# A hybrid decoder step on one core: sample sequences divided into front and back between mixed prompt items, with their products four heads beside each other

## What is computed

```python
s_c = einsum('bqkgd,bnkd->bqkgn', q, kc) * scale - sl * d_c      # compressed blocks
o_c = einsum('bqkgn,bnkd->bqkgd', masked_softmax(s_c), vc)
s_s = einsum('bqkgd,bqknld->bqkgnl', q, ks) * scale - sl * d_s   # selected blocks
o_s = einsum('bqkgnl,bqknld->bqkgd', masked_softmax(s_s), vs)
s_w = einsum('bqkgd,btkd->bqkgt', q, kw) * scale - sl * d_w      # window
o_w = einsum('bqkgt,btkd->bqkgd', masked_softmax(s_w), vw)
o = g[..., 0:1] * o_c + g[..., 1:2] * o_s + g[..., 2:3] * o_w    # gates
y = o @ w_o
```

## Time and profile before

| | us |
|---|---|
| median of 3 runs (1967.68 to 1974.69) | 1971.83 |
| the profiled execution, its own time | 1970.03 |
| its span, first to last instruction | 1968.4 |
| of this, the attention stage (1109.1 to 1441.3) | 332.2 |

### The profile page before, as it was taken

How to read it: one execution, slowest core, us unless ns; L and a number is a source line. 1 busy time by engine, 2 the same in 40 slices (tenths; PEclk the granted TensorE clock), 3 DMA queues, 4 the chain that set the end, 5 groups by cost and what they waited for, 6 DMA issues and landing times.

```text
span 1968.4 us, 30231 instructions
## 1 busy us (share of the span) xinstructions
PE 1714.8 (87%) x12401; PEld 1514.8 (77%) x12401; DVE 917.9 (47%) x1631; ACT 558.4 (28%) x1053; POOL 271.3 (14%) x384
## 2 busy tenths in 40 slices
PE   4789973579999999989898987878898999999995
PEld 2666652479999999979888754444487999999994
DVE  1489999664323222353234445544535323323333
ACT  2322221433221122222213533433423322122212
POOL 1003938020000000001100323232300000000000
PEclk7889986799999999998999988778688999999997
DMA  9399971061232223312312301010121223222311
GB/s 323 135 355 330 329 267 46 0 154 55 85 106 74 69 86 92 91 54 68 89 43 79 112 23 44 22 44 1 49 59 44 86 86 104 69 76 86 96 45 48
DMA packets 236591, 198.10 MB, mean 101 GB/s; under 512 B 6999, under 2 KB 196127, under 8 KB 236253
## 3 DMA queue, kind: packets, MB, share of 16 engines
q1 hardware_dynamic: 230448, 172.54, 28.5%
q0 software_dynamic: 5840, 23.30, 3.8%
q10 hardware_dynamic: 173, 0.39, 0.1%
HBM read 188.88 MB, written 11.20 MB: 102 GB/s over the span
## 4 chain that ended last, share of the span: by engine, by line
PE 70%; DVE 12%; issue 8%; ACT 4%; DMA 2%; DVEq 1%; POOL 1%; SPq 0%; ACTq 0%; POOLq 0%
PE ps L1422 56%; PE ps L1404 4%; PE ps L1730 3%; DVE y L1096 1%; PE ps L1806 1%; DMA ada<-in_w_ada_dram 1%; PE ps L1609 1%; DVE wl L950 1%; DVE r L1096 1%; PE ps L1450 1%; DVE Pp L1241 1%; DVE r L974 1%; ACT Pp L862 1%; POOL Pp L592 1%; PE ps L1694 1%
## 5 line engine op out<-in xcount | busy, mean ns | idle before, releaser
L1422 PE MATMUL ps<-Hh,wh 128*128 128x288 f32 x2128 | 469.5, 303 | 65.5 <-DVE Hl L989 40.8
L1422 PE MATMUL ps<-Hl,wh 128*128 128x288 f32 x2128 | 464.9, 301 | 0.0
L1422 PE MATMUL ps<-Hh,wl 128*128 128x288 f32 x2128 | 463.7, 300 | 0.0
L629 ACT ACTIVATE wh<-raw 128x1024 fp32r<-128x1024 f32 (+1 forms) x173 | 192.8, 1116 | 818.6 <-PE ps L1422 798.3
L1422 PEld LDWEIGHTS ps<-Hh,wh 128*128 128x128 f32 x2128 | 350.3, 193 | 69.5 <-issue 68.2
L1422 PEld LDWEIGHTS ps<-Hl,wh 128*128 128x128 f32 x2128 | 351.1, 193 | 0.2
L1422 PEld LDWEIGHTS ps<-Hh,wl 128*128 128x128 f32 x2128 | 350.5, 193 | 0.2
L950 DVE TENSOR_TENSOR wl<-raw,wh 128x1024 fp32r<-128x1024 f32 (+1 forms) x173 | 225.1, 1301 | 255.1 <-ACT wh L629 254.6
L1422 PE MATMUL ps<-al,wh 128*128 128x288 f32 x704 | 151.0, 296 | 0.0
L1422 PE MATMUL ps<-ah,wl 128*128 128x288 f32 x704 | 150.9, 296 | 0.0
L1422 PE MATMUL ps<-ah,wh 128*128 128x288 f32 x704 | 150.9, 296 | 0.0
(11 more groups left out here) (267 smaller groups left out, 2033.4 us busy)
## 6 DMA issues: line engine op xcount, KB each, us to landing
ada<-in_w_ada_dram SPq DMA_DIRECT2D x64, 1024.0 KB, 7.7
raw<-in_ffn_w_up_dram SPq DMA_DIRECT2D x88, 512.0 KB, 3.8
raw<-in_ffn_w_down_dram SPq DMA_DIRECT2D x32, 704.0 KB, 4.6
raw<-in_conv_w_pw_dram SPq DMA_DIRECT2D x24, 512.0 KB, 8.3
raw<-in_w_kv_dram SPq DMA_DIRECT2D x12, 512.0 KB, 3.8
C<-in_cache_kv_dram POOLq DMA_DIRECT2D x32, 128.0 KB, 4.3
raw<-in_nsa_w_in_dram SPq DMA_DIRECT2D x8, 512.0 KB, 3.8
Cs<-in_cache_kv_dram SPq DMA_DIRECT2D x16, 256.0 KB, 3.8
```

Source lines behind the costliest of these rows:

```text
L629: A(wh[:, u % RING, 0:K, 0:w], raw[:, u % RING, 0:K, 0:w], ACT.Copy).then_inc(hi_ready, 1)
L1422: last = M(ps[0:w, 2 * s + h, 0:HT], wt[:, s, k, 0:w], rt[:, k, h * HT:(h + 1) * HT], start=(k == 0 and i == 0), stop=(k == K - 1 and i == 2))
```

## The change

Three things change, all in the attention stage.

1. **The plan.** Prompt items come in a mixed order (`PROMPTS`; i = 1, 3, 3, 1, 1, 2, 3, 0, 3, 0, 2, 0, 2, 1, 2, 0). Sample sequences are no items of the pipeline any more: a front (`s_keys` twice, `s_score`, `s_weigh`) and a back (`s_turn` twice, `s_prod`, `s_oturn`) are placed each in the slot of a given prompt step (`SMP_FRONT`, `SMP_BACK`), spread among what is left of the item ahead after its first four entries. Those four stand one by one between the new item's four scores and `cmp`. `weigh` stands four entries later.
2. **The product.** The turned weights are stationary (32 columns), values move (64 columns), and four heads write 32 PSUM partitions each, beside each other. The result [128, 64] is copied to `So` (DVE), transposed back (`s_oturn`), and written to `oTs` in two copies by DVE or ACT.
3. **Buffers and the end.** `Cs` and `Cw` have three buffers. The sample columns are split at the last `s_oturn`, and the first three units of `w_o` at the last item's products 0 and 1 and the last `out`. SP still loads these units after the last `s_prod`, which now comes in step 15.

```diff
+PROMPTS = [(0, 1), (0, 3), (1, 3), (1, 1), (2, 1), (0, 2), (2, 3), (0, 0),
+           (3, 3), (1, 0), (1, 2), (2, 0), (2, 2), (3, 1), (3, 2), (3, 0)]
+SMP_FRONT = [2, 6, 7, 9, 10, 11, 12, 13]
+SMP_BACK = [3, 8, 8, 10, 12, 12, 14, 15]
...
+        seq = new[:1]
+        for k in range(1, len(new)):
+            seq += old[:1] + new[k:k + 1]
+            old = old[1:]
...
+        while n_old < len(old) or n_smp < len(smp):
+            if n_smp < len(smp) and (n_smp * max(len(old), 1) < n_old * len(smp) or n_old == len(old)):
+                rest.append(smp[n_smp])
...
+        if more:
+            rest.insert(4, ("weigh", j, 0))
...
-WO_AT = {ATT.index(("out", LAST_SMP + 1 + k, 0)): k for k in range(3)}
+SPLIT_WO = ATT.index(("s_oturn", NB - 1, 0))
+N_LAST = len(PROMPTS) - 1
+WO_AT = {ATT.index(("prod", N_LAST, 0)): 0, ATT.index(("prod", N_LAST, 1)): 1, ATT.index(("out", len(ITEMS) - 1, 0)): 2}
...
-                            sp.wait_ge(S("s_pv"), b - 1)
+                            sp.wait_ge(S("s_pv"), b - 2)
...
-                        for kp in range(2):
-                            src = ps[64 * kp:64 * kp + 64, 6 + n % 2, 384:448].rearrange("p (a e r t) -> p a e r t", a=2, e=2, r=2)
-                            for par in range(2):
-                                V.tensor_copy(dst[64 * par:64 * par + 64, :, kp], src[:, :, :, par])\
-                                    .then_inc(S("o_free") if kp and par else S("o_smp"), 1)
+                        V.tensor_copy(So[:], ps[:, 6 + n % 2, 384:384 + HD]).then_inc(S("o_free"), 1)
...
+                for x_ in range(7):
+                    for kv in range(NKV):
+                        o32 = slice(32 * kv, 32 * kv + 32)
+                        if x_ == 6:
+                            lhs, rhs = PTs[0:NCS, 6, o32], vc_s[:, b, kv, :]
+                        elif x_ % 3 == 2:
+                            lhs, rhs = PTs[0:TS, x_, o32], vrow[0:TS, 4, x_ // 3, kv, :]
+                        else:
+                            lhs, rhs = PTs[:, x_, o32], (Cs, Cw)[x_ // 3][b % 3][:, x_ % 3, 256 + 64 * kv:320 + 64 * kv]
+                        last = M(ps[o32, 6 + it % 2, 384:384 + HD], lhs, rhs, start=(x_ == 0), stop=(x_ == 6))
```

More of the change, by code:

```diff
@@ L101 @@
 RING_ADA = 3
[L104 to L108, removed]
+PROMPTS = [(0, 1), (0, 3), (1, 3), (1, 1), (2, 1), (0, 2), (2, 3), (0, 0),
+           (3, 3), (1, 0), (1, 2), (2, 0), (2, 2), (3, 1), (3, 2), (3, 0)]
+SMP_FRONT = [2, 6, 7, 9, 10, 11, 12, 13]
+SMP_BACK = [3, 8, 8, 10, 12, 12, 14, 15]
 def KVI(n):
-    return n // 4, 3 - n % 4
+    return PROMPTS[n]
 def _blocks(n):
@@ L119, in _blocks, with _back @@
     return [(2, 0)] + [(br, kb) for br in range(2) for kb in range(i + 1)]
[L122 to L132, removed]
+def _back(n):
     steps = len(_blocks(n))
@@ L140, in _attention_plan @@
 def _attention_plan():
[L142 to L165, removed]
@@ L166, in _attention_plan, with put @@
-    return plan
-ATT = _attention_plan()
+    plan, items = [], []
+    def put(m):
+        plan.append(m)
+        if m[0] == "s_prod" or m[0] == "prod" and m[2] == len(_blocks(m[1])) - 1:
+            items.append(("sample" if m[0] == "s_prod" else "prompt", m[1]))
+            plan.append(("out", len(items) - 1, 0))
+    for j in range(len(PROMPTS) + 1):
+        more = j < len(PROMPTS)
+        new = [("score", j, a) for a in range(4)] + [("cmp", j, 0)] if more else []
+        old = _back(j - 1) if j else [("s_gates", 0, 0), ("p_gates", 0, 0)] + [("vc", h, 0) for h in range(4)]
+        seq = new[:1]
+        for k in range(1, len(new)):
+            seq += old[:1] + new[k:k + 1]
+            old = old[1:]
+        smp = []
+        for b in range(NB):
+            if SMP_BACK[b] == j:
+                smp += [("s_turn", b, 0), ("s_turn", b, 1), ("s_prod", b, 0), ("s_oturn", b, 0)]
+        for b in range(NB):
+            if SMP_FRONT[b] == j:
+                smp += [("s_keys", b, 0), ("s_keys", b, 1), ("s_score", b, 0), ("s_weigh", b, 0)]
+        rest, n_old, n_smp = [], 0, 0
+        while n_old < len(old) or n_smp < len(smp):
+            if n_smp < len(smp) and (n_smp * max(len(old), 1) < n_old * len(smp) or n_old == len(old)):
+                rest.append(smp[n_smp])
+                n_smp += 1
+            else:
+                rest.append(old[n_old])
+                n_old += 1
+        if more:
+            rest.insert(4, ("weigh", j, 0))
+        for m in seq + rest:
+            put(m)
@@ L394, in turned, with smp_done @@
             eng.wait_ge(S("pt_act") if j % 2 else S("pt_dve"), j // 2 + 1)
+        def smp_done(eng):
+            for par in range(2):
+                mine = [b for b in range(NB) if TURN[("s_oturn", b, 0)] % 2 == par]
+                if mine:
+                    turned(eng, ("s_oturn", mine[-1], 0))
         block = ctx.enter_context(nc.Block())
@@ L891, in evacuate @@
                     A(PTs[0:TS, 3 * x_ + 2], src[0:TS, 256:384], ACT.Copy).then_inc(S("pt_act"), 1)
+                elif what == "s_oturn":
+                    q = src[0:HD, 0:P].rearrange("p (c r t) -> p c r t", c=DC, r=2)
+                    A(oTs[0:HD, :, NT * n:NT * n + NT], q[:, :, 0], ACT.Copy).then_inc(S("o_smp"), 1)
+                    A(oTs[HD:P, :, NT * n:NT * n + NT], q[:, :, 1], ACT.Copy).then_inc(S("pt_act"), 1)
             for at_, m in enumerate(ATT):
@@ L1275, in weights @@
                     V.tensor_tensor(z, z, maskc[:].unsqueeze(1).to_broadcast([P, G, NCP]), ALU.mult).then_inc(S("zmask"), 1)
-                    dve.wait_ge(S("zmask"), kv + 1)
+                    dve.wait_ge(S("zmask"), sum(KVI(k)[1] == 0 for k in range(n + 1)))
                 dve.wait_ge(W, 4 * n + 3)
```

63 lines of the change are left out of this document (33 added, 30 removed).

## The result

The changed kernel takes 1907.17 us (median of 4 runs, 1905.64 to 1908.03), against 1970.5 us for the kernel before on the same chip: a ratio of 0.9676, 95% interval 0.9656 to 0.9696. That is 63 us less, with 59 forecast. The profiled execution took 1907.56 us, with a span of 1905.9.

What follows compares the result with a forecast made beforehand. PE bounds the attention stage, losing time to idle and low clock. Work 203.9 x 1.105 = 225.3, plus 10, 9 and 4, gives 248.3 us; plus 25 of clock, 273, 59 less than 332.2: 1911 us, range 1878 to 1950.

Steps and rivals of the forecast that it cites:

- The division of the stage: Old attention stage of 332.2 us split into 56.9 idle, 60.3 clock loss and 214.9 work at full clock.
- The products: Eight sample products, four heads beside each other, fall from 3.02 to 1.3 us each at full clock, saving 13.8 us.
- The rival "not beside each other": Heads do not run beside each other where all 128 rows are used; products stay at 3.02 us, 1926 us; chance 10%.
- The work left: PE's attention-stage work at full clock: 214.9 less 13.8 for products plus 2.8 for turns back, 203.9 us.
- The ratio 1.105: Stage length over PE work in mixed steps, from the old stage's first 38.1 us; turns 203.9 into 225.3 us.
- POOL at short places: PE waits for POOL's scaling at five places behind short items, 2 us each, 10 us in all, bounds 0 to 23.
- Bare chains in steps 8, 10 and 12: Sample backs behind prompt items with i = 0 leave PE waiting, 3 us a step, 9 us in all, bounds 0 to 14.
- The end: Stage end: late `w_o` loads and splits make the dense units start 4.8 us after the last product, 4 us more.
- The clock: Five low-clock stretches in the stage in place of twelve, at 5.0 us each, costing 25 us.
- The rival with the clock as bad as before: Twelve low-clock stretches remain in the stage, costing 60.3 us, giving 1946 us; chance 17%.
- that of no fall at all: Slots fill the last bare places and no low-clock stretch is left: stage 248.3 us, 1886 us; chance 14%.
- late weights at every item: Later `weigh` makes PE wait at all 15 item boundaries, 4.6 us idle and 5.0 clock each: 1986 us; chance 5%.

Runs made afterwards that it cites:

- e4: The kernel before with 64 unused float32 matmuls added, eight at each hand-over through a sample: 1949.18 us, ratio 0.9883 to the kernel before.
- e1: The changed kernel's plan and buffers with the sample product as before (two heads beside each other, no turn back): 1920.38 us, ratio 0.9737 to the kernel before.
- e2: The kernel before's plan with the four-head sample product and its turn back two entries later: 1953.24 us, ratio 0.9903 to the kernel before.
- e3: The changed kernel with the last two sample backs, and so the loads of `w_o`, one step earlier: 1910.35 us, ratio 0.9689 to the kernel before.
- e5: The changed kernel with three unused matmuls ahead of each of sample products 1 to 5: 1903.49 us, ratio 0.9639 to the kernel before.
- e6: The e3 kernel with the three `w_o` splits moved earlier, to products of the last two items: 1908.90 us, ratio 0.9690 to the kernel before.
- e9: The changed kernel with two buffers for `Cs` and `Cw` in place of three: 1905.89 us, ratio 0.9665 to the kernel before.
- e10: The changed kernel with sample backs one a step and, behind items with i = 0, the first sample turn earlier: 1912.25 us, ratio 0.9691 to the kernel before.
- e11: The e5 kernel with 14 more unused matmuls in the two waits at the stage's end: 1904.81 us, ratio 0.9651 to the kernel before.
- e8: The changed kernel with `weigh` another four entries later: 1911.23 us, ratio 0.9715 to the kernel before.
- e7: The changed kernel with prompt items in the old order (kv by kv, i from 3 to 0): 1917.96 us, ratio 0.9737 to the kernel before.

## Why the prediction was right, and where its terms were off

The time (1911 against 1907), the range and the mechanism held: the gain is the clock and the idle of the hand-overs, through PE always having prompt work at a sample entry. e4 shows that the clock is a cause and not an accompaniment, and e1 that the plan carries most. That the number came so near is partly luck. By the division of the forecast, work was 8 us too low, idle 14 too high and the clock 3 too high, and 6 us from outside the stage hid most of what was left. Point by point:

- **The division of the stage.** 56.9 idle, 60.3 clock: the two together became 52 us. This reading of the kernel before was the step that made the forecast. Its idle stands. Its clock was some 8 us too high and its work as much too low, because PE's busy time at 0.50 was halved where a factor of 1.75 is measured in that kernel (1.69 to 1.77 in all). "All eight sample products end with the clock down" holds for seven: the one at 1216.67 runs at 1.00 throughout, and the clock falls 1.4 us after its end.
- **The products.** Forecast 1.3 us each, measured 1.46. The old product of 3.02 us was not wholly at full clock, since the clock fell at 1316.5, ahead of its end at 1316.96; in e1 and e4 it takes 2.83 us at 1.00 from its start to the next instruction's. So 8 x (2.83 - 1.46) = 11.0 us are saved where 13.8 stood. The Trainium skill (TensorE: Matmul & The Clock Gate, section LDWEIGHTS) gave 1.5 as an estimate and was nearer than the row at 0.11 us; but its formula gives 26.7 ns a load, and the sixteen records of 128 rows take 22.5 ns each, so the total agrees better than its parts. By the rows at 1365.26 sixteen records of 128 rows take 0.36 us from start to start, so 0.18 for eight where I took 0.11; seven such groups are 1.26 us, and the changes of height add 0.20 where I took 0.50. The line took 14.7 us in all, not "about 10": three of the eight products run wholly at 0.50, at 2.34 us each. The rival "not beside each other" is out: e1's line has 26.4 us, the changed kernel's 14.7.
- **The work left.** Forecast 203.9, measured 211.6 to 213.3 by the same halving. By own price it went from 223.0 to 215.1 or 215.8, so it fell by 7 to 8 us where 13.8 - 2.8 = 11.0 stood: the larger error is the 214.9 at the start. The product saved 3 us less than forecast. The eight turns back took 1.5 us of PE where 2.8 stood. The plan added 1 to 3 us, which I had at nothing. It has more changes of form (row height, or transpose to product): 358 in e1 against 334 before, 323 against 296 in e2. At the 0.10 us that I took for one, these are some 2.5 us; that they are the cause is not shown.
- **The ratio 1.105.** The longest piece of the changed kernel at full clock, windows over steps before 8:

```profile
1121.10:1237.10 116.00, 107.07 (x879) 56.31 (x879) 87.37 (x290) 69.03 (x203) 51.66 (x70) 1.00 0.12 34
```

  It takes 116.0 / 107.07 = 1.083 times PE's work, with transposes and products in turn; transposes are 39.2 of the 107.1 us. It also answers the rival drawn from the Trainium skill (TensorE: Matmul & The Clock Gate, section on PE-mode transpose), that transposes don't count as busy and so bring the clock down in every mixed step: the clock stays at 1.00 for 116 us. It is not safe there, though. The second execution of the same kernel falls once in this piece, in step 7, and e3, e5, e6, e9, e10 and e11 do so too. Window of the second execution:

```profile
1216.00:1219.40 3.40, 3.40 (x16) 2.24 (x15) 2.77 (x10) 0.65 (x3) 0.74 (x2) 0.50 0.00 0
```

- **The three extras.** POOL at short places: 10 forecast, 1.2 measured; e8 shows that four more entries of delay would cost little. Bare chains in steps 8, 10 and 12: in the places named, with waits of 1.61, 0.72, 1.34 and 0.72 us for `PTs`, 1.44 for `oTs` and 1.7 for `So`, 7.5 us against 9. A wait of 1.67 us for `nmin` in step 11 was not named. The end: 1.19 + 3.18 = 4.4 us against the 4.8 forecast, and the dense units start 11.2 us after the last sample product where 11.0 stood. I took the loads for its cause; e3 shows that most of it is splits behind one another and e6 that it is also the output's chain. In all idle is 30.0 us, where 248.3 - 203.9 = 44.4 stood: 9 us of the difference are POOL, the rest mostly the ratio.
- **The clock.** 25 us forecast at five places, four of them named; 21.9 and 15.8 measured by halves in two executions (18 and 13 by own price), at six places each: the stage's very start, steps 8, 10, 11 and 12 and the end in the one; the start, steps 7, 8, 11 and 12 and the end in the other.
- **Outside the stage.** "Nothing should differ": the span less the stage went from 1636.2 to 1642.4 us. This is not the change: with the same code ahead of it, the stage began anywhere from 1109.0 (e3) to 1117.2 (e7). It hid part of an error: the stage was 9.5 us shorter than forecast, and the time only 3.4.

The rival with the clock as bad as before is refuted by the windows, that of no fall at all by the same, late weights at every item by 1.2 us of waiting for POOL.

What stays open: what exactly starts a low stretch in steps 7 to 12. Filling the wait in front of one took that stretch away (e5, e11), halving the wait did not (e10), and in step 7 the same instructions with the same waits (about 0.5 and 0.8 us) have a stretch behind them in one profile of the changed kernel and none in the other.

## What to carry to other kernels

Divide a PE-bound stage into idle, clock loss and work at full clock before pricing a change; here the work hardly changed and some 61 to 65 us went from the other two. Price the work in a low stretch by the same kinds of record at full clock, not by halving. An item with little work of its own should not be a stage of the pipeline but be laid in pieces between the pieces of a large one, and the cost of the finer mixture (here 1 to 3 us) belongs in the sum. Whether low clock is a cause can be asked directly: put unused matmuls into the idle places and see whether the kernel gets faster.

## What the runs showed of the hardware

- Adding 38.6 us of PE busy time made the kernel 24 us faster, as the clock of the stage rose from 0.78 to 0.94.
- At a granted clock of 0.50 these float32 matmuls took less than twice as long as at 1.00: a sample product 2.34 us against 1.53, a prompt product's four records 1.12 against 0.65, a stage's mix 1.69 to 1.77 times.
- The same program has low stretches of different length from one execution to another: at step 8 one of 20.5 us in the first profile of the changed kernel, one of 3.4 us in the second, behind the same instructions. In this last one the stage was 5 us shorter. So a single profile prices the clock at one place only roughly. The runs scatter too: e5 and e11 by 15 and 14 us, the changed kernel by 2 in its first set and 7 in its second.
- Float32 matmuls with four targets of 32 columns beside each other and all 128 rows: 16 records of 64 columns in 0.36 us, a whole product of 56 records in 1.46 us. Eight records take 0.24 to 0.25 us at 64 and at 15 rows, the change of height included: fewer rows are no cheaper.
